# Stick-breaking attention: the products of a pair's two heads taken in turns instead of one head behind the other

## The reference, cut to what matters

```python
def stick_breaking_attention(q, k, v):
    ...
        z = jnp.einsum('bqhd,bkhd->bhqk', qb, k).astype(jnp.float32) * scale
        strict = kpos[None, :] < qpos[:, None]
        log_one_minus = jnp.where(strict, -jax.nn.softplus(z), 0.0)
        suffix = lax.cumsum(log_one_minus, axis=3, reverse=True) - log_one_minus
        w = jnp.where(strict, jnp.exp(jax.nn.log_sigmoid(z) + suffix), 0.0)
        return jnp.einsum('bhqk,bkhd->bqhd', w.astype(v.dtype), v)
```

## Time and profile before

| | |
|---|---|
| median of 3 runs | 2954.04 us |
| profiled execution: time | 2952.2 us |
| profiled execution: span | 2950.9 us |
| TensorE matmul busy | 2434.6 us, 83% |
| VectorE busy | 1099.7 us, 37% |
| ScalarE busy | 811.9 us, 28% |
| mean granted clock of TensorE | 0.914 of full |

### The profile page before, as it was taken

One profiled execution on the slowest core, in us unless ns is written; L12 is line 12 of the kernel. 1 busy time (PEld: TensorE's weight loads), 2 busy tenths in 40 slices (PEclk: granted clock), 3 DMA queues, 4 the chain that ended last, 5 costly groups with the idle time before them and its releaser, 6 DMA issues.

```text
span 2950.9 us, 31836 instructions
## 1 busy us (share of the span) xinstructions
PE 2434.6 (83%) x13622; PEld 1559.3 (53%) x13622; DVE 1099.7 (37%) x1874; ACT 811.9 (28%) x1143; POOL 3.2 (0%) x7
## 2 busy tenths in 40 slices
PE   7877766767876676768999888799999998987999
PEld 5542111114542111118977454589899774545897
DVE  3741000104630010005554334655455453446554
ACT  3230000002520000005443332444344333324443
POOL 0000000000000000000000000000000000000000
PEclk9978888889888988899999899999999998999999
DMA  9669999998369999997543242456655422514562
GB/s 314 242 238 421 421 422 421 422 421 297 133 261 421 421 422 421 422 404 205 179 157 113 72 131 84 129 143 186 186 157 186 152 91 72 157 58 129 157 180 92
DMA packets 346418, 703.68 MB, mean 238 GB/s; under 512 B 15651, under 2 KB 230947, under 8 KB 296998
## 3 DMA queue, kind: packets, MB, share of 16 engines
q1 hardware_dynamic: 346278, 701.65, 65.4%
HBM read 700.56 MB, written 1.05 MB: 238 GB/s over the span
## 4 chain that ended last, share of the span: by engine, by line
PE 61%; DMA 26%; DVE 7%; ACT 5%; issue 1%; SPq 1%; DVEq 0%; ACTq 0%
PE psum L727 59%; DMA ring<-in_moe_w_up 12%; DMA ring<-in_moe_w_down 7%; DMA ring<-in_moe_w_gate 6%; PE psum L731 2%; DVE arena L1870 1%; ACT ring L1427 1%; DVE lent_r L1870 1%; ACT lent_r L1427 1%; ACT arena L1427 1%; DVE arena L1878 1%; SPq L597 1%; DVE arena L1881 1%; ACT xn L1427 0%; DMA ring<-in_ada_w 0%
## 5 line engine op out<-in xcount | busy, mean ns | idle before, releaser
L727 PE MATMUL psum<-ring,arena 128*32 128x512 f32 (+3 forms) x3672 | 667.4, 660 | 268.4 <-DMA ring<-in_moe_w_up 102.2
L727 PE MATMUL psum<-lent_r 128*128 128x256 f32 (+1 forms) x3440 | 636.7, 299 | 14.7 <-DVE lent_r L1870 14.7
L727 PEld LDWEIGHTS psum<-ring,arena 128*32 128x32 f32 (+2 forms) x3672 | 185.8, 129 | 752.3 <-issue 258.0
L727 PEld LDWEIGHTS psum<-lent_r 128*128 128x128 f32 x3440 | 550.7, 195 | 34.5 <-DVE lent_r L1870 12.1
L727 PE MATMUL psum<-arena_r,lent_r 128*128 128x256 f32 (+1 forms) x1888 | 519.0, 316 | 17.5 <-DVE lent_r L1870 9.2
L1870 DVE TENSOR_TENSOR lent_r<-ring,lent_r 128x2048 fp32r<-128x2048 f32 (+1 forms) x158 | 349.3, 2211 | 282.4 <-ACT lent_r L1427 282.3
L727 PEld LDWEIGHTS psum<-arena_r,lent_r 128*128 128x128 f32 x1888 | 366.9, 195 | 40.7 <-DVE arena_r L1870 10.2
L1427 ACT ACTIVATE arena<-psum 128x512 f32<-128x512 f32 (+3 forms) x118 | 67.9, 597 | 982.3 <-PE psum L727 913.0
L1427 ACT ACTIVATE lent_r<-ring 128x2048 fp32r<-128x2048 f32 (+1 forms) x158 | 289.9, 1839 | 157.5 <-PE psum L727 157.1
L727 PE MATMUL psum<-ring,hT 128*128 128x512 f32 (+1 forms) x576 | 268.1, 601 | 3.8 <-ACT arena L1427 2.7
L727 PE MATMUL psum<-lent_r,arena_r 128*128 128x512 f32 x1056 | 241.5, 390 | 0.4
(11 more groups left out here) (143 smaller groups left out, 1501.1 us busy)
## 6 DMA issues: line engine op xcount, KB each, us to landing
ring<-in_moe_w_gate SPq DMA_DIRECT2D x128, 1024.0 KB, 23.5
ring<-in_moe_w_up SPq DMA_DIRECT2D x128, 1024.0 KB, 23.2
ring<-in_moe_w_down SPq DMA_DIRECT2D x128, 1024.0 KB, 24.1
ring<-in_ffn_wi SPq DMA_DIRECT2D x176, 512.0 KB, 5.1
ring<-in_ada_w SPq DMA_DIRECT2D x48, 1024.0 KB, 7.9
ring<-in_w_in SPq DMA_DIRECT2D x46, 1024.0 KB, 5.2
ring<-in_ffn_wo SPq DMA_DIRECT2D x44, 1024.0 KB, 4.9
ring<-in_w_out SPq DMA_DIRECT2D x8, 1024.0 KB, 4.9
```

The source lines that it names most:

```text
L727: return T.matmul(out, lhsT, rhs, start=start, stop=stop, **kw)
```

## The change

In `logits` the four products go by key tile and then by head. In the suffix stage the first logits of both heads come first, then the four products with tri and ones, then the second logits of both heads, then the last two products with tri. In PV both heads' first products precede both heads' second products. Every product keeps its operands, its bank and its place within its head; no wait and no signal is added or removed, and the signal stays on the last product of each stage. The other engines' programs are unchanged.

```diff
--- before.py
+++ after.py
@@ -1132,13 +1132,20 @@
                 o = 64 * j
                 return mx.skT[o:o + 64, n, :], mx.sqT[o:o + 64, n, :]
 
+            def logits_of(bank, n, j, kt, stop):
+
+                kk, qq = head_pair(n, j)
+                if kt == 0:
+                    return mm(psum[:, bank, 0:S], kk[:, 0:P], qq, True, stop)
+                return mm(psum[:, bank, S:3 * P], kk[:, P:S], qq[:, P:S], True, stop)
+
             def logits(n):
                 if n:
                     T.wait_ge(*E.sb_sp.at(l, n - 1))
-                for j in range(2):
-                    kk, qq = head_pair(n, j)
-                    mm(psum[:, j, 0:S], kk[:, 0:P], qq, True, True)
-                    i = mm(psum[:, j, S:3 * P], kk[:, P:S], qq[:, P:S], True, True)
+
+                for kt in range(2):
+                    for j in range(2):
+                        i = logits_of(j, n, j, kt, True)
                 i.then_inc(*E.sb_pe.inc(l, "z", n))
 
             logits(0)
@@ -1148,23 +1155,25 @@
                 if n:
                     T.wait_ge(*E.sb_o.at(l, n - 1))
                 for j in range(2):
-                    b = 2 + j
-                    kk, qq = head_pair(n, j)
-                    mm(psum[:, b, 0:S], kk[:, 0:P], qq, True, False)
-                    mm(psum[:, b, 0:S], tri, mx.sp[:, j, 0:S], False, False)
-                    mm(psum[:, b, P:S], ones, mx.sp[:, j, S:3 * P], False, True)
-                    mm(psum[:, b, S:3 * P], kk[:, P:S], qq[:, P:S], True, False)
-                    i = mm(psum[:, b, S:3 * P], tri, mx.sp[:, j, S:3 * P], False, True)
+                    logits_of(2 + j, n, j, 0, False)
+                for j in range(2):
+                    mm(psum[:, 2 + j, 0:S], tri, mx.sp[:, j, 0:S], False, False)
+                    mm(psum[:, 2 + j, P:S], ones, mx.sp[:, j, S:3 * P], False, True)
+                for j in range(2):
+                    logits_of(2 + j, n, j, 1, False)
+                for j in range(2):
+                    i = mm(psum[:, 2 + j, S:3 * P], tri, mx.sp[:, j, S:3 * P], False, True)
                 i.then_inc(*E.sb_pe.inc(l, "suffix", n))
                 if n < 3:
                     logits(n + 1)
                 yield
                 T.wait_ge(*E.sb_w.at(l, n))
+                out = [psum[64 * j:64 * j + 64, 2, 0:S] for j in range(2)]
+                v_of = [slice((2 * n + j) * HD, (2 * n + j + 1) * HD) for j in range(2)]
                 for j in range(2):
-                    h = 2 * n + j
-                    out = psum[64 * j:64 * j + 64, 2, 0:S]
-                    mm(out, mx.sv[:, 0, h * HD:(h + 1) * HD], mx.z[:, j, 0:S], True, False)
-                    i = mm(out[:, P:S], mx.sv[:, 1, h * HD:(h + 1) * HD], mx.z[:, j, S:3 * P], False, True)
+                    mm(out[j], mx.sv[:, 0, v_of[j]], mx.z[:, j, 0:S], True, False)
+                for j in range(2):
+                    i = mm(out[j][:, P:S], mx.sv[:, 1, v_of[j]], mx.z[:, j, S:3 * P], False, True)
                 i.then_inc(*E.sb_pe.inc(l, "pv", n))
                 yield
```

## The result

The changed kernel takes 2927.0 us (median of 6 runs, 2922.41 to 2931.39) against 2953.65 us for the kernel before (6 runs): ratio 0.9913, 95% interval 0.99 to 0.9927, some 26 us less. I had forecast 15.5 us less, 2938.5 us, and a range down to 2930. The profiled execution took 2927.39 us with a span of 2926.1 us.

A forecast was written before the change was run, and what follows sets the result against it. TensorE held 61% of the chain, with the suffix stages on it. Savings of 7.8 us in layer 0 and 7.7 in layer 1 gave 2954.0 - 15.5 = 2938.5 us, with an 8-in-10 range of 2930 to 2947 us.

The forecast's parts named there:

- Stage A: The stretch of each mixer where stick-breaking runs; forecast 7 to 8 us shorter in each layer.
- The sum within the stage: Suffix stage of one pair: 3.19 us against 4.62 at full clock, 5.89 against 8.34 at half clock.
- its two terms: Suffix stage, full clock: four fewer 64-row/128-row passages (0.8 us), and 0.43 + 0.21 us of streaming side by side.
- Logits and PV at 0: Logits and PV stages: heads already overlap, so no gain; bounds 0.64 us loss each to at most 0.2 gain.
- Cover for VectorE's late addition: Pair 0's mask addition moves up only 0.4 us, at no cost; without cover each pair 0 loses up to 2.1 us.
- The clock: Pair 1's half-clock stretch, about 13 us, assumed to end as long after the fillers' start as before; otherwise gain 11.1 us.
- rival 3: One or two half-clock stretches in stage A shorten or vanish: 5 to 12 us more gain, 2926 to 2933 us; chance 0.09.
- each place gives up to 6.5 us more: Extra gain wherever half clock ends sooner or does not begin, in one or two of four half-clock pairs.
- rival 1: Suffix stage: only passages go, heads' logits don't run side by side; 7.9 us gain, 2946 us; chance 0.06.
- rival 2: VectorE's or ScalarE's order or a late transfer hides part of the gain: 2944 to 2948 us; chance 0.08.
- rival 4: Clock also falls to half in pairs 2 and 3: slower, 2958 us with three new stretches; chance 0.04.
- rival 5: Nothing changes, as the engine already takes up head 1's first logits early: 2954 us; chance 0.03.

The follow-up runs named there:

- e5: Changed kernel with head 1's suffix-stage 64-row products reading head 0's q and k, so no side-by-side overlap; one execution of 2943.24 us, not compared.
- e4: Kernel before with only logits and PV taking the heads in turns, all suffix stages in the old order: 2951.65 us, ratio 1.0001.
- e6: Kernel before plus unread products in TensorE's waits ahead of the suffix stages, 4 for pair 0 and 8 for pair 1: 2934.31 us, ratio 0.9949.
- e9: Changed kernel plus three extra tri products at the start of the suffix stages of pairs 0 and 1: 2934.66 us, ratio 0.9955.
- e7: Changed kernel plus unread products in the waits ahead of the suffix stages of pairs 0 and 1: 2924.83 us, ratio 0.9912 to the kernel before.
- e3: Kernel before with the new order only in the suffix stage of pair 1: 2946.05 us, ratio 0.9976.
- e10: The changed kernel as it is, measured again in another job: 2928.16 us, ratio 0.9928 to the kernel before.
- e8: Changed kernel with tri and ones products first, then all 64-row logits of both heads and the next pair's: 2926.58 us, ratio 0.9924 to before.

## Why the prediction was wrong

- That the suffix stages are on the path and that all of their saving reaches the end: right. Stage A became 28.3 us shorter and the program 26. I had written that each stage A must be 7 to 8 us shorter; it was 13.5 and 14.8, and the miss lies there.
- The sum within the stage: right to some hundredths (3.20 and 5.86 us against 3.19 and 5.89), and e5 confirms its two terms at full clock, 0.78 for the passages and 0.64 for the overlap.
- Logits and PV at 0: right (e4). Cover for VectorE's late addition: right.
- The step that failed is the paragraph "The clock": "My 2.45 us assumes that it ends as long after the fillers' start as before", and for pair 0 that the half clock begins as before. I took the half-clock stretch as given, cut only by the work removed, and so priced pair 0 at 2.5 and 2.4 us and pair 1 at 2.45. Measured in the traces: 6.2 and 7.7 us, and 4.5 and 4.6. Of the 28.3 us in stage A, 15.5 are the forecast's and nearly 13 come from full clock where I had kept half clock. e6 shows that the clock alone is worth that much: the old order with the waits filled is 13 to 15 us faster. e9 shows where the assumption fails: the clock's return does not wait for the fillers; a dense suffix stage has it back before its own end. That the passages, and not the overlap, do this is argued and not shown: e5's two layers differ.
- The rivals: rival 3 (the clock gives more, 2926 to 2933 us) is the one that happened, and 2927.0 lies in it. I gave it 0.09 and cut the range at 2930. Its own term, "each place gives up to 6.5 us more", should have set the low end: with three of the four places it reaches 2919. The trace of the changed kernel refutes rival 1 (first logits 0.63 us, not 1.05), rival 2 (the exponential does not wait for the addition), rival 4 (the suffix stages of pairs 2 and 3 at 1.00) and rival 5 (3.20 us against 4.62).
- What I could have read: in the trace of before, layer 0, pair 0 fell to half clock after a wait of 2.06 us and stayed there through a suffix stage that leaves 1.6 of 4.6 us without streaming, while the fillers behind it brought full clock back. That a change which takes half of those pauses out may shorten the stretch deserved more than 0.09. Some 50 us at half clock stood in the two stages; at full clock they would take 25 us less, more than the whole sum of 15.5.

## What to carry to other kernels

When a change thins out pauses in a TensorE stage that runs at half clock, price the half-clock stretch itself as a term, at half its length, and let it set the range; the forecast from full-clock instruction times is only the sure part. In this kernel matmuls of 64 rows on the two halves of the array run beside each other without any turn-taking in the program, as long as nothing of another form stands between them (eight records in 0.85 us); so group products by form first, and by head second. Two to four microseconds of idle time ahead of a stage can cost more behind it than they last: products that nobody reads, put into waits of 2.06 and 3.85 us in both layers (11.8 us in all), made the old order 13 to 15 us faster (and the new order no faster, e7).

## What the runs showed of the hardware that I had not expected

- Products of two heads overlap against program order: eight records of 64 rows take 0.85 us from start to start, whether the heads alternate or stand behind each other (e4, no difference in time), and head 1's products of 256 columns start ahead of head 0's of 128.
- The granted clock in pair 0 differs between executions of one order: in the old order from 1.00 (e3, layer 0) to 0.63 (before, layer 1) over the stretch up to PV.
- How long TensorE stayed at half clock behind the wait of 3.85 us differed with the order of the work behind it: in the old order full clock was back 12.3 to 12.9 us behind the stage's start (eight stretches), in the new one after 5.4 to 6.1 (seven of eight: the changed kernel, e3, e9, e10) and once after 8.4 (e10, layer 1). In one trace (e8, layer 0) pair 1 was at full clock behind the same wait.
